# The last 256 inner columns of each expert, computed with the weights stationary and the rows moving

## The chip, the cores and the metric

The kernel runs on one core of a Trainium2 chip. The time is device microseconds of one execution. Three executions of the kernel before took 1574.29, 1574.44 and 1581.74 us; the median is 1574.44 us.

The engines are named as the profile names them: PE is the TensorE matmul stream, PEld its stream of weight loads, DVE is VectorE, ACT is ScalarE, POOL is GpSimd, SP is SyncE, whose queue issues the weight transfers.

## The reference, cut to what matters

The reference is one step of a two-layer decoder trunk for 256 prompt rows and 32 sample rows of width 1024. The second layer ends with a top-2-of-8 expert SwiGLU, and only that part is touched here:

```python
D_MODEL = 1024
D_FF = 2816
N_EXPERTS = 8
TOP_K = 2

def _swiglu(h, wg, wu, wd):
    return (jax.nn.silu(h @ wg) * (h @ wu)) @ wd

def _moe(h, router, wg, wu, wd):
    xt = h.reshape(-1, D_MODEL)
    logits = (xt @ router).astype(jnp.float32)
    top_v, top_i = lax.top_k(logits, TOP_K)
    top_w = jax.nn.softmax(top_v, axis=-1)
    gates = jnp.sum(jax.nn.one_hot(top_i, N_EXPERTS, dtype=jnp.float32) * top_w[..., None],
                    axis=1).astype(h.dtype)
    y = jnp.zeros_like(xt)
    for e in range(N_EXPERTS):
        y = y + gates[:, e:e + 1] * _swiglu(xt, wg[e], wu[e], wd[e])
    return y.reshape(shp)
```

Everything is float32. The inner width 2816 is five blocks of 512 columns and a rest of 256.

## The kernel before

Each expert works on at most 96 gathered rows (`CAP`). Each expert's weights come in 33 pieces of 1 MB (128 partitions x 2048 elements); `g` counts all 264 pieces, `i` is the piece within the expert. Pieces 0 to 19 are four pieces for each 512-column block: two halves of the gate weights, two halves of the up weights. Piece 20 is the gate weights of the last 256 columns, piece 21 the up weights of the same columns, both with all 8 blocks of 128 input rows. Pieces 22 to 32 are the down weights, 256 inner rows each.

To keep the accuracy of float32 at the speed of the rounded type float32r, every operand is split into a high part and a low rest: ACT copies a piece from the ring `ering` (8 slots) into `wH` (3 slots), DVE subtracts and writes `wL`. Each product is then three matmuls, high x high, high x low and low x high (`product`). The matmuls of one piece are issued in the order of its input blocks.

The order of the work is written out by hand. In each engine's program a loop runs over the pieces, and tables of piece numbers say behind which piece the small steps come: `SILU_AT` (ACT takes the gate sums out of PSUM bank 0 through Silu into `sgE`), `MULT_AT` (DVE multiplies bank 1, the up sums, with `sgE` into `hS`), `TRANSPOSE_AT` (PE transposes `hS` in blocks of 128 columns into bank 6 or 7, function `e_hidden`), `HID_AT` (ACT copies the transposed block as the high part into `hH`, DVE writes the low rest to `hL`). The down products use `hH` and `hL` as stationary operands and wait for `e_hl`. ACT makes the high part of piece g+2 in its step g, after piece g-1 is done, DVE the low part after it, and SP issues the transfer of piece g+8 once the low part of piece g is made (line 483).

In pieces 0 to 21 the 96 rows are the stationary operand (`xgH`, `xgL`, 128x96) and the weights move through, 512 or 256 columns at a time, so the sums come out as 96 rows x columns; that is why `hS` has to be transposed. The last block has two blocks of 128 inner columns, and its two transposes come behind piece 22.

Names of rows in the profile: line 2355 is the matmul in `product`, 2364 the transposes of `hS`, 2347 the transposes of the gathered rows, 1044 ACT's high part, 1546 DVE's low part, 1080 the Silu, 1664 the multiplication, 1085 and 1670 the high and low part of the hidden block.

Of the kernel before, what the change touches and what calls it, by code (L numbers as in the profile page):

```python
# [19 lines left out]
ALU = mybir.AluOpType  # L20
ACT = mybir.ActivationFunctionType
# [6 lines left out]
P = 128  # L28
D, DC = 1024, 8
# [9 lines left out]
E_, CAP = 8, 96  # L39
# [10 lines left out]
HRING = 3  # L50
# [4 lines left out]
def trunk_kernel(nc, a, out):  # L55

    with ExitStack() as ctx:
        def sb(name, shape, dt=F32):
            return ctx.enter_context(nc.sbuf_tensor(name, shape, dt))
# [4 lines left out]
        banks = [ctx.enter_context(nc.psum_tensor(f"bank{i}", [P, 512], F32)) for i in range(8)]  # L64
# [55 lines left out]
        wH = sb("wH", [P, HRING, SLOT], F32R)  # L120
        wL = sb("wL", [P, HRING, SLOT], F32R)
        with nc.sbuf_tensor("hrow", [P, 4, D], F32) as hrow:
            hrow = hrow[:, 1:4, :]
        hH, hL = [sb(name, [P, FC, CAP], F32R) for name in ("hH", "hL")]
# [4 lines left out]
        xgH, xgL = [sb(name, [P, DC, 2 * CAP], F32R) for name in ("xgH", "xgL")]  # L129
# [1 line left out]
        emem = sb("emem", [P, 1024])  # L131
        xtk = sb("xtk", [P, 3, D])
        yS = sb("yS", [P, D])
        sgE = sb("sgE", [P, 512])[0:CAP]
        outg = sb("outg", [P, D])
        hS = sb("hS", [P, 2, 512])[0:CAP]
        Sx = sb("Sx", [P, 3, 2 * CAP])
        Dh = nc.dram_tensor("token_rows", (T, D), F32, kind="Internal").ap()
        Dy = nc.dram_tensor("expert_rows", (E_ * CAP + 1, D), F32, kind="Internal").ap()
# [136 lines left out]
        S = {}  # L276
# [25 lines left out]
        for n in range(16):  # L302
            q = (n + 8) % 16
# [24 lines left out]
        for m, i in enumerate((1, 2, 0)):  # L328
            w = a["b_w_rkv"][0, i].rearrange("(k p) n -> p k n", p=P)
# [156 lines left out]
        SILU_AT = (2, 6, 10, 14, 18, 21)  # L486
        MULT_AT = (4, 8, 12, 16, 20, 22)
        HID_AT = (6, 10, 14, 18, 21, 23)
        TRANSPOSE_AT = (5, 9, 13, 17, 20, 22)
        BON = (6, 7, 0, 1, 2, 3, 6, 7)  # L490
        GATE_AT = (0, 4, 8, 12, 16, 20)
        UP_AT = (2, 6, 10, 14, 18, 21)
# [2 lines left out]
        def main(rd):  # L495
            return isinstance(rd, int)
# [297 lines left out]
        def _(act):  # L794
# [271 lines left out]
            def e_round(rd):  # L1066
                e_w_high(rd, 0)
                e_w_high(rd, 1)
                e_x_high(rd, 0)
                for g in range(ALL):  # L1070
                    e, i = g // EPIECES, g % EPIECES
                    if i == 0 and e:
                        e_result(rd, e - 1)
                    if i in SILU_AT:
                        q = SILU_AT.index(i)
                        act.wait_ge(S["e_piece"], rd * ALL + g)
                        if not main(rd) or 6 * e + q:
                            act.wait_ge(S["e_he"], rd * 6 * E_ + (6 * e + q))
                        w = 512 if q < 5 else 256
                        s_.activation(sgE[:, 0:w], banks[0][0:CAP, 0:w], ACT.Silu).then_inc(S["e_sg"], 1)  # L1080
                    if i in HID_AT:
                        q = HID_AT.index(i)
                        nb = 4 if q < 5 else 2
                        act.wait_ge(S["e_htr"], rd * 6 * E_ + (6 * e + q + 1))
                        s_.activation(hH[:, 4 * q:4 * q + nb, :], banks[6 + q % 2][:, 0:nb * CAP]
                                      .rearrange("p (j s) -> p j s", j=nb), ACT.Copy).then_inc(S["e_hh"], 1)
                    if i == 27 and e < E_ - 1:
                        e_x_high(rd, e + 1)
                    if main(rd) and e == LAST and i == 10:
                        act.wait_ge(S["last_sx"], 4)  # L1090
                        s_.activation(SwT, banks[2][0:CAP, 0:T], ACT.Copy).then_inc(S["last_sx"], 1)
                    if main(rd) and e == LAST and i == 24:
                        s_.activation(w7[:, 2, 0:1], eps[:, 0:1], ACT.Sqrt)
                        act.wait_ge(S["e_yout"], 16 * LAST)
                    if g + 2 < ALL:
                        e_w_high(rd, g + 2)
                if not main(rd):
                    e_result(rd, E_ - 1)
# [48 lines left out]
        def _(dve):  # L1147
# [497 lines left out]
            def e_round(rd):  # L1645
                if not main(rd):
                    e_slots(rd, 0)
                    e_index(rd, 0)
                e_w_low(rd, 0)
                e_w_low(rd, 1)  # L1650
                e_x_low(rd, 0)
                c_index(rd)
                for g in range(ALL):
                    e, i = g // EPIECES, g % EPIECES
                    if i == 0 and e:
                        e_result(rd, e - 1)
                    if i in MULT_AT:
                        q = MULT_AT.index(i)
                        w = 512 if q < 5 else 256
                        dve.wait_ge(S["e_piece"], rd * ALL + g)  # L1660
                        dve.wait_ge(S["e_sg"], rd * 6 * E_ + (6 * e + q + 1))
                        if not main(rd) or 6 * e + q >= 2:
                            dve.wait_ge(S["e_htr"], rd * 6 * E_ + (6 * e + q - 1))
                        v.tensor_tensor(hS[:, q % 2, 0:w], banks[1][0:CAP, 0:w], sgE[:, 0:w], ALU.mult) \
                            .then_inc(S["e_he"], 1)
                    if i in HID_AT:
                        q = HID_AT.index(i)
                        nb = 4 if q < 5 else 2
                        dve.wait_ge(S["e_hh"], rd * 6 * E_ + (6 * e + q + 1))
                        v.tensor_tensor(hL[:, 4 * q:4 * q + nb, :], banks[6 + q % 2][:, 0:nb * CAP]  # L1670
                                        .rearrange("p (j s) -> p j s", j=nb), hH[:, 4 * q:4 * q + nb, :].bitcast(F32),
                                        ALU.subtract).then_inc(S["e_hl"], 1)
                    if i == 5 and e < E_ - 1:
                        e_slots(rd, e + 1)
                    if i == 9 and e < E_ - 1:
                        e_index(rd, e + 1)
                    if main(rd) and e == LAST:
                        if i == 5:
                            last_slots()
                        if i in ADD_AT:  # L1680
                            add_got(ADD_AT.index(i))
                    if i == 27 and e < E_ - 1:
                        e_x_low(rd, e + 1)
                    if g + 2 < ALL:
# [42 lines left out]
        def _(pe):  # L1727
# [624 lines left out]
            def product(dst, lhs, rhs, start, stop):  # L2352

                for m, (l, r) in enumerate(((0, 0), (0, 1), (1, 0))):
                    mm = t.matmul(dst, lhs[l], rhs[r], start=(start and m == 0), stop=(stop and m == 2),  # L2355
                                  skip_group_check=True)
                return mm

            def e_hidden(rd, e, q):
                pe.wait_ge(S["e_he"], rd * 6 * E_ + (6 * e + q + 1))  # L2360
                if not main(rd) or 6 * e + q >= 2:
                    pe.wait_ge(S["e_hl"], rd * 6 * E_ + (6 * e + q - 1))
                for j in range(4 if q < 5 else 2):
                    mm = t.transpose(banks[6 + q % 2][:, CAP * j:CAP * j + CAP], hS[:, q % 2, P * j:P * j + P],  # L2364
                                     ident[0:CAP, 0:CAP])
                mm.then_inc(S["e_htr"], 1)
# [28 lines left out]
            def e_round(rd):  # L2395
# [3 lines left out]
                for g in range(ALL):  # L2399
# [9 lines left out]
                        pe.wait_ge(S["e_ya"], rd * E_ + e)  # L2409
                        pe.wait_ge(S["e_yd"], rd * E_ + e)  # L2410
                    pe.wait_ge(S["e_lo"], rd * ALL + (g + 1))
                    if i < 22:
                        kn, half = (4, i % 2) if i < 20 else (DC, 0)
                        b, w = ((i % 4) // 2, 512) if i < 20 else (i - 20, 256)
                        w2 = [x[:, g % HRING, :].rearrange("p (k n) -> p k n", k=kn) for x in (wH, wL)]
                        for k in range(kn):
                            kk = kn * half + k
                            mm = product(banks[b][0:CAP, 0:w], [x[:, kk, o:o + CAP] for x in (xgH, xgL)],
                                         [x[:, k, :] for x in w2], kk == 0, kk == DC - 1)
                    else:  # L2420
                        r = i - 22
                        pe.wait_ge(S["e_hl"], rd * 6 * E_ + (6 * e + r // 2 + 1))
                        if main(rd) and e == LAST and i >= 31:
                            mm = last_down(g)
                            if i == 32:
                                mm.then_inc(S["e_piece"], 2)
                            continue
                        for k in range(2):
                            for hf in range(2):
                                mm = down(g, k, hf)  # L2430
# [47 lines left out]
```

## Time and profile before

| | |
|---|---|
| median of three executions | 1574.44 us |
| span of the profiled execution | 1580.4 us |
| highest of the three executions, the one nearest to that span | 1581.74 us |
| PE busy / share of the span | 1531.4 us, 97% |
| DVE busy / share | 1075.8 us, 68% |
| ACT busy / share | 843.9 us, 53% |
| expert stage, first to last product | 808 to 1569 us of the span |
| transfers in the expert stage | 360 to 400 GB/s |

The busy share of PE is made of durations whose ends are modelled: the matmuls overlap, and a matmul of 512 columns that is shown with 0.39 us starts every 0.23 us. What a matmul costs is therefore read from the distance of two starts, not from its duration. The same holds for weight loads in PEld.

### The profile page before, as it was taken

The page shows a single profiled execution, that of the slowest core. Times are in us where ns is not written, and L with a number is a line of the kernel's source. Part 1 is how long each engine was busy: PE and PEld are TensorE (multiplying, and loading weights), DVE is VectorE, ACT ScalarE, POOL GpSimd, SP SyncE. Part 2 cuts the span into 40 slices and gives each one's busy share as a digit, 9 for nine tenths or more (in the row PEclk, how much of TensorE's full clock was granted, in tenths as well). Part 3 has the DMA queues.
Part 4 walks back from the last instruction along what each step waited for, and adds up shares of the span by engine and source line. Part 5 has one row for each costly group of instructions (what it writes and reads, how often), then busy time and mean ns, then how long its engine had stood idle before and what let it go on. Part 6 is the DMA issues. An engine that isn't in the chain of part 4 may idle for free.

```text
span 1580.4 us, 27011 instructions
## 1 busy us (share of the span) xinstructions
PE 1531.4 (97%) x11783; PEld 1252.3 (79%) x11783; DVE 1075.8 (68%) x1038; ACT 843.9 (53%) x813; POOL 129.2 (8%) x169
## 2 busy tenths in 40 slices
PE   7999999999899989999879999999999999999997
PEld 7999999999777789986657777777777777777774
DVE  5696465544506564212378888888988889888997
ACT  5444443333223322223167777777777777777775
POOL 0074100000100030123100000000000000000010
PEclk9999999999999999889879999999999999999999
DMA  8552675445243020024099999999999999999992
GB/s 265 171 154 63 177 224 162 152 129 160 82 136 107 27 57 4 20 49 133 2 360 381 396 379 400 382 370 363 380 385 377 369 373 383 380 368 373 385 388 99
DMA packets 249472, 377.96 MB, mean 239 GB/s; under 512 B 27401, under 2 KB 141305, under 8 KB 249058
## 3 DMA queue, kind: packets, MB, share of 16 engines
q1 hardware_dynamic: 247106, 370.04, 67.2%
q0 software_dynamic: 2032, 6.05, 1.2%
q8 instruction: 95, 1.56, 0.4%
q14 instruction: 31, 0.25, 0.1%
q10 hardware_dynamic: 208, 0.07, 0.0%
HBM read 368.34 MB, written 7.78 MB: 238 GB/s over the span
## 4 chain that ended last, share of the span: by engine, by line
PE 93%; DVE 5%; ACT 1%; issue 1%; DMA 0%; ACTq 0%; DVEq 0%
PE bank L2355 46%; PE bank L1761 23%; PE bank L1884 5%; PE bank L2030 2%; PE bank L2277 1%; PE bank L2015 1%; PE bank L2286 1%; PE bank L2364 1%; PE bank L2226 1%; PE bank L1814 1%; DVE wL L1546 1%; PE bank L2168 1%; PE bank L2296 1%; PE bank L2217 0%; PE bank L2159 0%
## 5 line engine op out<-in xcount | busy, mean ns | idle before, releaser
L1546 DVE TENSOR_TENSOR wL<-ering,wH 128x2048 fp32r<-128x2048 f32 x264 | 603.4, 2289 | 86.6 <-ACT wH L1044 85.4
L1044 ACT ACTIVATE wH<-ering 128x2048 fp32r<-128x2048 f32 x264 | 505.8, 1917 | 148.1 <-PE bank L2355 148.0
L2355 PE MATMUL bank<-wH,xgH 128*96 128x512 f32 (+1 forms) x768 | 290.4, 378 | 1.4 <-DVE xgL L1553 1.4
L2355 PE MATMUL bank<-wH,xgL 128*96 128x512 f32 (+1 forms) x768 | 287.3, 374 | 0.0
L2355 PE MATMUL bank<-wL,xgH 128*96 128x512 f32 (+1 forms) x768 | 287.2, 374 | 0.0
L2355 PEld LDWEIGHTS bank<-wH,xgH 128*96 128x96 f32 x768 | 124.4, 162 | 44.3 <-DVE xgL L1553 1.7
L2355 PEld LDWEIGHTS bank<-wH,xgL 128*96 128x96 f32 x768 | 124.4, 162 | 44.1
L2355 PEld LDWEIGHTS bank<-wL,xgH 128*96 128x96 f32 x768 | 124.6, 162 | 41.5
L2355 PE MATMUL bank<-wH,hH 128*96 128x512 f32 x352 | 139.5, 396 | 0.3 <-DVE wL L1546 0.3
L2355 PE MATMUL bank<-wH,hL 128*96 128x512 f32 x352 | 138.3, 393 | 0.0
L2355 PE MATMUL bank<-wL,hH 128*96 128x512 f32 x352 | 137.9, 392 | 0.0
L868 ACT ACTIVATE fwH<-fring 128x2048 fp32r<-128x2048 f32 (+1 forms) x38 | 64.2, 1690 | 116.6 <-PE bank L1761 116.6
L1263 DVE TENSOR_TENSOR fwL<-fring,fwH 128x2048 fp32r<-128x2048 f32 (+1 forms) x38 | 76.4, 2010 | 42.5 <-ACT fwH L868 42.5
L1761 PE MATMUL bank<-fxH,fwH 128*128 128x288 f32 x352 | 104.4, 297 | 0.0
L1761 PE MATMUL bank<-fxH,fwL 128*128 128x288 f32 x352 | 103.8, 295 | 0.0
L1761 PE MATMUL bank<-fxL,fwH 128*128 128x288 f32 x352 | 103.5, 294 | 0.0
L1884 PE MATMUL bank<-arena 128*128 128x288 f32 (+1 forms) x416 | 101.9, 406 | 0.0
L1884 PEld LDWEIGHTS bank<-arena 128*128 128x128 f32 (+1 forms) x416 | 77.5, 187 | 23.4 <-issue 0.8
L1761 PE MATMUL bank<-inH,inW 128*128 128x288 f32 x256 | 76.9, 300 | 1.0 <-DVE inL L1209 0.6
L2355 PEld LDWEIGHTS bank<-wH,hL 128*96 128x96 f32 x352 | 56.7, 161 | 24.7
L2355 PEld LDWEIGHTS bank<-wH,hH 128*96 128x96 f32 x352 | 56.8, 161 | 24.3 <-DVE wL L1546 1.1
L1761 PE MATMUL bank<-inH,lowW 128*128 128x288 f32 x256 | 75.5, 295 | 0.0
(405 smaller groups left out, 2468.6 us busy)
## 6 DMA issues: line engine op xcount, KB each, us to landing
ering<-m_w_gate SPq DMA_DIRECT2D x88, 1024.0 KB, 8.0
ering<-m_w_up SPq DMA_DIRECT2D x88, 1024.0 KB, 8.6
ering<-m_w_down SPq DMA_DIRECT2D x88, 1024.0 KB, 8.3
arena<-a_w_in SPq DMA_DIRECT2D x16, 1024.0 KB, 5.8
arena<-b_w_rkv SPq DMA_DIRECT2D x12, 1024.0 KB, 5.3
fring<-f_w_gate SPq DMA_DIRECT2D x11, 1024.0 KB, 5.4
fring<-f_w_up SPq DMA_DIRECT2D x11, 1024.0 KB, 5.3
fring<-f_w_down SPq DMA_DIRECT2D x16, 704.0 KB, 4.7
```

The costliest lines, as they stand in the source:

```text
L868: nc.scalar.activation(fw[n % FRING][0][:, 0:w], fring[:, (F_GU + n) % RING, 0:w], ACT.Copy) \
L1044: s_.activation(wH[:, g % HRING, :], ering[:, g % MRING, :], ACT.Copy).then_inc(S["e_hi"], 1)
L1263: v.tensor_tensor(fw[n % FRING][1][:, 0:w], fring[:, (F_GU + n) % RING, 0:w], fw[n % FRING][0][:, 0:w].bitcast(F32), ALU.subtract).then_in ...
L1546: v.tensor_tensor(wL[:, g % HRING, :], ering[:, g % MRING, :], wH[:, g % HRING, :].bitcast(F32), ALU.subtract).then_inc(S["e_lo"], 1)
L1761: mm = t.matmul(bank[:, 0:T], w2[l], x2[r][:, k, :], start=(start and m == 0), stop=(stop and m == 2))
L1814: mm = t.matmul(banks[c % 4][:, t0:t0 + n], vtok[0:n, i, P * c:P * c + P], w, start=False, stop=True, skip_group_check=True)
L1884: mm = t.matmul(bank, w(k), x[:, k, :], start=(k == 0), stop=(k == ks - 1))
L2015: mm = t.matmul(banks[3 * f][ch, 64 * j:64 * j + 64], MS[ch, BL, i, 8 * f + j, :], X[ch, 8 * f + j, :], start=(j == 0), stop=True, skip_gr ...
L2030: mm = t.matmul(banks[1 + 3 * f + x][ch, 64 * j:64 * j + 64], pair[x], pair[1 - x], start=(j == 0), stop=True, skip_group_check=True)
L2168: mm = t.matmul(out_[ch, :, NS * b:NS * b + NS], S0[p][ch, b, :], QR[ch, p, :, NP_ + NS * b:NP_ + NS * b + NS], start=(p % 4 == 0 and b == ...
L2226: mm = t.matmul(bank[BOTH[h2], 64 * b:64 * b + 64], S0[p][BOTH[h2], b, :], id64[BOTH[h2]], start=False, stop=True, skip_group_check=True)
L2355: mm = t.matmul(dst, lhs[l], rhs[r], start=(start and m == 0), stop=(stop and m == 2), skip_group_check=True)
```

## The change

Pieces 20 and 21 of each expert are computed the other way round. A block of 128 x 128 weights (`wH` or `wL`) is now the stationary operand and the 96 rows (`xgH` or `xgL`) move through. The sums come out as 128 inner columns x 96 rows, two such blocks side by side in the bank, which is the layout that `hH` and `hL` need. So the Silu and the multiplication of the last block run on 128x192 instead of 96x256, the two transposes behind piece 22 go, and ACT and DVE make `hH` and `hL` of this block from `hS` in SBUF instead of from PSUM. The counter `e_htr` runs to 5 per expert instead of 6, and the waits on it are renumbered.

```diff
-        TRANSPOSE_AT = (5, 9, 13, 17, 20, 22)
+        TRANSPOSE_AT = (5, 9, 13, 17, 20)
...
+                        else:
+                            s_.activation(sgF5[:, 0:2 * CAP], banks[0][:, 0:2 * CAP], ACT.Silu).then_inc(S["e_sg"], 1)
...
+                        else:
+                            act.wait_ge(S["e_he"], rd * 6 * E_ + (6 * e + 6))
+                            s_.activation(hH[:, 20:22, :], hS2[:, 1, 0:2 * CAP].rearrange("p (j s) -> p j s", j=2), ACT.Copy) \
+                                .then_inc(S["e_hh"], 1)
...
-                        if not main(rd) or 6 * e + q >= 2:
-                            dve.wait_ge(S["e_htr"], rd * 6 * E_ + (6 * e + q - 1))
+                        if q >= 2:
+                            dve.wait_ge(S["e_htr"], rd * 5 * E_ + (5 * e + q - 1))
+                        elif q == 0 and (not main(rd) or e):
+                            dve.wait_ge(S["e_htr"], rd * 5 * E_ + 5 * e)
+                        elif q and (not main(rd) or e):
+                            dve.wait_ge(S["e_hl"], rd * 6 * E_ + 6 * e)
...
+                            v.tensor_tensor(hS2[:, 1, 0:2 * CAP], banks[1][:, 0:2 * CAP], sgF5[:, 0:2 * CAP], ALU.mult) \
+                                .then_inc(S["e_he"], 1)
...
-                for j in range(4 if q < 5 else 2):
+                for j in range(4):
...
-                    if i < 22:
-                        kn, half = (4, i % 2) if i < 20 else (DC, 0)
-                        b, w = ((i % 4) // 2, 512) if i < 20 else (i - 20, 256)
-                        w2 = [x[:, g % HRING, :].rearrange("p (k n) -> p k n", k=kn) for x in (wH, wL)]
-                        for k in range(kn):
-                            kk = kn * half + k
-                            mm = product(banks[b][0:CAP, 0:w], [x[:, kk, o:o + CAP] for x in (xgH, xgL)],
-                                         [x[:, k, :] for x in w2], kk == 0, kk == DC - 1)
...
+                    elif i < 22:
+                        w2 = [x[:, g % HRING, :].rearrange("p (k n) -> p k n", k=DC) for x in (wH, wL)]
+                        for j in range(2):
+                            for k in range(DC):
+                                mm = product(banks[i - 20][:, CAP * j:CAP * j + CAP], [x[:, k, P * j:P * j + P] for x in w2],
+                                             [x[:, k, o:o + CAP] for x in (xgH, xgL)], k == 0, k == DC - 1)
```

In PE's program, where piece 20 begins behind the last 512-column matmuls of the first expert, the order before reads (name of the moving operand first where two stand behind the arrow, then the shape of the result):

```order
L2355 MATMUL bank<-wH,xgH 96x512
L2355 MATMUL bank<-wL,xgH 96x512
L2355 MATMUL bank<-wH,xgL 96x512
L2355 MATMUL bank<-wH,xgH 96x256 [waits e_lo,e_sg]
L2355 MATMUL bank<-wL,xgH 96x256
L2355 MATMUL bank<-wH,xgL 96x256
```

And now:

```order
L2370 MATMUL bank<-wH,xgH 96x512
L2370 MATMUL bank<-wL,xgH 96x512
L2370 MATMUL bank<-wH,xgL 96x512
L2370 MATMUL bank<-xgH,wH 128x96 [waits e_lo,e_sg]
L2370 MATMUL bank<-xgL,wH 128x96
L2370 MATMUL bank<-xgH,wL 128x96
```

The waits stay where they were. A piece had 24 matmuls of 256 moving columns there, and has 48 of 96 moving columns now; the same holds for piece 21.

Behind piece 22, the first of the down weights, PE's program before has the two transposes, with their wait for the multiplication (`e_he`) and for the buffer (`e_hl`):

```order
L2355 MATMUL bank<-wL,hH 96x512
L2355 MATMUL bank<-wH,hL 96x512
L2364 MATMUL bank<-ident,hS 128x96 [waits e_hl,e_he]
L2364 MATMUL bank<-ident,hS 128x96
L2355 MATMUL bank<-wH,hH 96x512 [waits e_hl,e_lo]
L2355 MATMUL bank<-wL,hH 96x512
```

Now piece 23 follows piece 22 at once:

```order
L2370 MATMUL bank<-wL,hH 96x512
L2370 MATMUL bank<-wH,hL 96x512
L2370 MATMUL bank<-wH,hH 96x512 [waits e_hl,e_lo]
L2370 MATMUL bank<-wL,hH 96x512
L2370 MATMUL bank<-wH,hL 96x512
```

On DVE and ACT the steps stand in the same places as before; only their shapes and sources differ.

## Rows read from the trace of the kernel before

**Rows 1.** Chain that ended last, from the page: share of the span.
```profile
PE 93%; DVE 5%; ACT 1%; issue 1%; DMA 0%; ACTq 0%; DVEq 0%
```

**Rows 2.** Stretches: length, busy PE, PEld, DVE, ACT, POOL (count), clock, DMA share, GB/s.
```profile
813.00:873.79 60.79, 60.79 (x305) 44.66 (x303) 51.64 (x35) 46.10 (x33) 0.91 (x1) 1.00 1.05 385
867.88:873.79 5.91, 5.91 (x54) 5.90 (x52) 5.27 (x5) 4.55 (x4) 0.00 (x0) 1.00 1.02 408
```

**Rows 3.** Waits from 800 us on: who waited for whom, us, times, longest.
```profile
ACT wH L1044 <- PE bank L2355: 148.0, 194, 4.4
...
PE bank L2355 <- DVE wL L1546: 0.3, 1, 0.3
```

**Rows 4.** Timeline of PE, first expert, pieces 20 and 21: start, length.
```profile
867.88 0.28 PE L2355 MATMUL bank<-wH,xgH 128*96 128x256 f32 x1
...
870.67 0.49 PE L2364 MATMUL bank<-ident,hS 96*128 96x96 f32 x4
870.95 0.34 PE L2355 MATMUL bank<-wH,xgH 128*96 128x256 f32 x1
871.12 0.27 PE L2355 MATMUL bank<-wL,xgH 128*96 128x256 f32 x1
...
873.79 0.39 PE L2355 MATMUL bank<-wH,hH 128*96 128x512 f32 x1
```

**Rows 5.** The same of the second expert: start of piece 20, start of piece 22.
```profile
961.99 0.28 PE L2355 MATMUL bank<-wH,xgH 128*96 128x256 f32 x1
...
968.06 0.39 PE L2355 MATMUL bank<-wH,hH 128*96 128x512 f32 x1
```

**Rows 6.** Weight loads of the whole span by form: busy, mean ns of one, idle before.
```profile
L2355 PEld LDWEIGHTS bank<-wL,xgH 128*96 128x96 f32 x768 | 124.6, 162 | 41.5
...
L1761 PEld LDWEIGHTS bank<-fxL,fwH 128*128 128x128 f32 x352 | 66.3, 188 | 0.0
...
L2364 PEld LDWEIGHTS bank<-ident,hS 96*128 96x128 f32 x176 | 20.0, 141 | 6.4 <-DVE hS L1664 0.2
```

**Rows 7.** Timeline of PEld: float32r loads right behind each other, first 128, then 96 columns.
```profile
137.87 0.19 PEld L1810 LDWEIGHTS bank<-bsH,onesR 128*128 128x128 f32 x1
137.98 0.19 PEld L1811 LDWEIGHTS bank<-bsL,onesR 128*128 128x128 f32 x1
...
870.92 0.16 PEld L2355 LDWEIGHTS bank<-wH,xgH 128*96 128x96 f32 x1
871.00 0.17 PEld L2355 LDWEIGHTS bank<-wL,xgH 128*96 128x96 f32 x1
```

**Rows 8.** Timeline of PE: 128-column float32 loads with 8 moving columns each.
```profile
791.50 0.37 PE L2315 MATMUL bank<-emem,ones 128*128 128x8 f32 x2
791.72 0.37 PE L2315 MATMUL bank<-emem 128*128 128x8 f32 x2
```

**Rows 9.** Timeline of PE, first expert, the two transposes behind piece 22.
```profile
876.56 0.33 PE L2364 MATMUL bank<-ident,hS 96*128 96x96 f32 x2
876.67 0.46 PE L2355 MATMUL bank<-wH,hH 128*96 128x512 f32 x1
876.97 0.39 PE L2355 MATMUL bank<-wL,hH 128*96 128x512 f32 x1
877.20 0.39 PE L2355 MATMUL bank<-wH,hL 128*96 128x512 f32 x1
```

**Rows 10.** Timeline of PE, last expert, down weights.
```profile
1561.09 0.40 PE L2355 MATMUL bank<-wH,hL 128*96 128x512 f32 x1
1561.76 0.48 PE L2355 MATMUL bank<-wH,hH 128*96 128x512 f32 x1 [0.28 <-DVE wL L1546]
```

**Rows 11.** Timeline of PE: transposes of the gathered rows, 128 stationary and 96 moving columns.
```profile
1451.24 0.83 PE L2347 MATMUL bank<-ident,xrow 96*128 96x96 f32 x8
1451.85 0.45 PE L2355 MATMUL bank<-wH,hH 128*96 128x512 f32 x1
```

**Rows 12.** Timeline of PE at 778 us, and its stretch with the granted clock.
```profile
778.08 7.95 PE L2296 MATMUL bank<-arena 128*128 128x8 f32 x48 [6.60 <-DVE arena L388]
...
778.10:785.80 7.70, 7.70 (x47) 7.68 (x48) 0.00 (x0) 0.00 (x0) 0.00 (x0) 0.50 0.00 0
```

More of the change, by code:

```diff
@@ L133, in trunk_kernel @@
         yS = sb("yS", [P, D])
-        sgE = sb("sgE", [P, 512])[0:CAP]
+        sgF5 = sb("sgE", [P, 512])
+        sgE = sgF5[0:CAP]
         outg = sb("outg", [P, D])
-        hS = sb("hS", [P, 2, 512])[0:CAP]
+        hS2 = sb("hS", [P, 2, 512])
+        hS = hS2[0:CAP]
         Sx = sb("Sx", [P, 3, 2 * CAP])
@@ L1078, in e_round @@
                             act.wait_ge(S["e_he"], rd * 6 * E_ + (6 * e + q))
-                        w = 512 if q < 5 else 256
-                        s_.activation(sgE[:, 0:w], banks[0][0:CAP, 0:w], ACT.Silu).then_inc(S["e_sg"], 1)
+                        if q < 5:
+                            s_.activation(sgE, banks[0][0:CAP, :], ACT.Silu).then_inc(S["e_sg"], 1)
+                        else:
+                            s_.activation(sgF5[:, 0:2 * CAP], banks[0][:, 0:2 * CAP], ACT.Silu).then_inc(S["e_sg"], 1)
                     if i in HID_AT:
                         q = HID_AT.index(i)
[L1083 to L1086, printed above, removed]
+                        if q < 5:
+                            act.wait_ge(S["e_htr"], rd * 5 * E_ + (5 * e + q + 1))
+                            s_.activation(hH[:, 4 * q:4 * q + 4, :], banks[6 + q % 2][:, 0:4 * CAP]
+                                          .rearrange("p (j s) -> p j s", j=4), ACT.Copy).then_inc(S["e_hh"], 1)
+                        else:
+                            act.wait_ge(S["e_he"], rd * 6 * E_ + (6 * e + 6))
+                            s_.activation(hH[:, 20:22, :], hS2[:, 1, 0:2 * CAP].rearrange("p (j s) -> p j s", j=2), ACT.Copy) \
+                                .then_inc(S["e_hh"], 1)
                     if i == 27 and e < E_ - 1:
@@ L1658, in e_round @@
                         q = MULT_AT.index(i)
-                        w = 512 if q < 5 else 256
                         dve.wait_ge(S["e_piece"], rd * ALL + g)
                         dve.wait_ge(S["e_sg"], rd * 6 * E_ + (6 * e + q + 1))
-                        if not main(rd) or 6 * e + q >= 2:
-                            dve.wait_ge(S["e_htr"], rd * 6 * E_ + (6 * e + q - 1))
-                        v.tensor_tensor(hS[:, q % 2, 0:w], banks[1][0:CAP, 0:w], sgE[:, 0:w], ALU.mult) \
-                            .then_inc(S["e_he"], 1)
+                        if q >= 2:
[4 more added lines that the diff above has]
+                            dve.wait_ge(S["e_hl"], rd * 6 * E_ + 6 * e)
+                        if q < 5:
+                            v.tensor_tensor(hS[:, q % 2, :], banks[1][0:CAP, :], sgE, ALU.mult).then_inc(S["e_he"], 1)
+                        else:
+                            v.tensor_tensor(hS2[:, 1, 0:2 * CAP], banks[1][:, 0:2 * CAP], sgF5[:, 0:2 * CAP], ALU.mult) \
+                                .then_inc(S["e_he"], 1)
                     if i in HID_AT:
@@ L1668, in e_round @@
                         nb = 4 if q < 5 else 2
+                        src = banks[6 + q % 2] if q < 5 else hS2[:, 1]
                         dve.wait_ge(S["e_hh"], rd * 6 * E_ + (6 * e + q + 1))
-                        v.tensor_tensor(hL[:, 4 * q:4 * q + nb, :], banks[6 + q % 2][:, 0:nb * CAP]
+                        v.tensor_tensor(hL[:, 4 * q:4 * q + nb, :], src[:, 0:nb * CAP]
                                         .rearrange("p (j s) -> p j s", j=nb), hH[:, 4 * q:4 * q + nb, :].bitcast(F32),
@@ L2411, in e_round @@
                     pe.wait_ge(S["e_lo"], rd * ALL + (g + 1))
-                    if i < 22:
-                        kn, half = (4, i % 2) if i < 20 else (DC, 0)
-                        b, w = ((i % 4) // 2, 512) if i < 20 else (i - 20, 256)
-                        w2 = [x[:, g % HRING, :].rearrange("p (k n) -> p k n", k=kn) for x in (wH, wL)]
-                        for k in range(kn):
-                            kk = kn * half + k
-                            mm = product(banks[b][0:CAP, 0:w], [x[:, kk, o:o + CAP] for x in (xgH, xgL)],
-                                         [x[:, k, :] for x in w2], kk == 0, kk == DC - 1)
+                    if i < 20:
+                        w2 = [x[:, g % HRING, :].rearrange("p (k n) -> p k n", k=4) for x in (wH, wL)]
+                        for k in range(4):
+                            kk = 4 * (i % 2) + k
+                            mm = product(banks[(i % 4) // 2][0:CAP, :], [x[:, kk, o:o + CAP] for x in (xgH, xgL)],
+                                         [x[:, k, :] for x in w2], kk == 0, kk == DC - 1)
+                    elif i < 22:
[4 more added lines that the diff above has]
+                                             [x[:, k, o:o + CAP] for x in (xgH, xgL)], k == 0, k == DC - 1)
                     else:
```

## The prediction, made before the changed kernel ran

> **What bounds the kernel now.** I read the chain of work that ended last first. It is PE for 93% of the span [rows 1], so PE is the engine to count on unless the stage of the change is another case. The stretches say it is not: from 813 to 873.79 us, the first expert at full clock, PE is busy for the whole 60.79 us, DVE for 51.64 and ACT for 46.10 [rows 2]. Modelled ends could hide a gap there, so I read the waits next. ACT waits 148.0 us for PE to free the `wH` slots, and PE waits 0.3 us in all for DVE's low parts [rows 3]. The transfers run at 385 GB/s, but nothing in the stage waits for them. So PE is the bound and the others follow. Whatever PE's stream of matmuls gets longer or shorter by in pieces 20 and 21 is what the kernel gets longer or shorter by, eight times over.
>
> What the reader is to see in the timeline is the pace. Piece 20 of the first expert starts at 867.88 us and the transposes behind it at 870.67: 24 matmuls in 2.79 us, 0.116 us each, with 256 moving columns, 0.45 ns a column. The weight load in front of each is shown with 162 ns [rows 6], more than that pace, so loads and matmuls overlap, and with 256 columns the moving side sets the pace. The question of this change is which side sets it when the stationary operand grows from 96 to 128 columns and the moving one shrinks from 256 to 96.
>
> **What goes.** In the first expert the stretch from piece 20 to piece 22 is 873.79 - 867.88 = 5.91 us [rows 4]; in the second 968.06 - 961.99 = 6.07 us [rows 5]. The eight experts alternate between these two, mean 5.99. The four transposes between the pieces take 870.95 - 870.67 = 0.28 us, and the first matmul behind them 0.17 instead of 0.12 (871.12 - 870.95) [rows 4]; these 0.33 us stay. So 48 matmuls cost 5.66 us an expert, and they go.
>
> The two transposes behind piece 22 go too: from 876.56 to 876.97 is 0.41 us for them and one matmul of 512 columns, which else takes 0.23 (877.20 - 876.97) [rows 9]. That is 0.18 us an expert, 1.4 us in all.
>
> **What comes.** 96 matmuls an expert instead of 48, each with its own load of 128 float32r columns. The moving side would take 96 x 0.45 = 0.044 us. The load takes longer. The trace has no float32r matmul with fewer than 256 moving columns, so the cost of the pair is bounded from the nearest rows:
> - Two float32r loads that stand right behind each other start 0.11 us apart with 128 columns (137.87 and 137.98) and 0.08 us apart with 96 (870.92 and 871.00) [rows 7]. The load port is free again after that time, though a load is shown with 188 and 162 ns [rows 6].
> - Plain float32 matmuls with 128-column loads and only 8 moving columns, so nothing on the moving side, go at (791.72 - 791.50)/2 = 0.11 us [rows 8].
> - The lowest pace of a pair of the new shape (128 stationary, 96 moving) is that of the transposes: 8 in 1451.85 - 1451.24 = 0.61 us, 0.076 us each [rows 11]. But their load is a different one: 141 ns for 128 columns where the float32r load takes 188 [rows 6].
> - The upper end is a load that hides behind nothing: 0.11 + 0.044 = 0.154 us.
>
> I take 0.111 us: it is the only pace that two independent places show for a load of this size, and the moving 0.044 us fits under it. 96 x 0.111 = 10.66 us, against 5.66: +5.00 us an expert, +40.0 us in all. A quarter of the moving columns is saved (9216 instead of 12288), but they are no longer what the time goes by; twice as many and a third wider loads are.
>
> **What lies beside it and costs nothing.** The Silu, the multiplication and the two halves of `hH` and `hL` change shape on ACT and DVE; those engines have 15 and 9 us to spare in 61 [rows 2], and longer pieces 20 and 21 give them more. The wait of ACT for `e_he` instead of `e_htr` stands in front of its high part of piece 25 only; the multiplication it waits for is made by DVE as soon as piece 21 and the Silu are done, and the first down piece that reads this block is the eleventh, piece 32, nine pieces of about 2.8 us later. If that cover were gone the cost would be one ACT step, under 1 us an expert. The renumbered waits on `e_htr` and `e_hl` are for things done pieces earlier. SP issues its transfers by DVE's low parts, so while pieces 20 and 21 take 5.3 us instead of 2.8 it slows down; the ring holds eight pieces and the stage was not waiting for transfers.
>
> In the last expert PE is once held up by DVE's low part: 1561.76 - 1561.09 = 0.67 us instead of 0.23 [rows 10], since DVE also adds the gathered results there. Five more microseconds in pieces 20 and 21 let DVE catch up: -0.4 us.
>
> **The sum.** +40.0 - 1.4 - 0.4 = +38.2 us. The rows come from an execution with a span of 1580.4 us, which lies 1.3 us under the highest of the three times, 1581.74; for that execution the sum gives 1619.9. The stage of the change had full clock throughout, so the sum is the same for the others, and on the median of 1574.4 it gives 1612.6 us. I say 1612.
>
> The Trainium skill, "TensorE: Matmul & The Clock Gate", section "Back-to-back issue gap", gives a sustained 81 ns for each pair of load and matmul at 128 columns. Of the float32r load the trace shows another figure, 0.11 us for 128 columns [rows 7]. By the page's 81 ns the pieces would take 7.8 us an expert, and the kernel would end near 1590 us, in the neighbourhood of the first rival.
>
> **Rivals.**
> - *The pair goes at the pace of the transposes, 0.076 us.* 96 x 0.076 = 7.3 us, +1.6 - 0.18 an expert, +11 us in all: about 1586 us. For it: the same shape. Against it: the loads of the transposes are shown 47 ns shorter than float32r ones with as many columns [rows 6], and two float32r loads are 0.11 us apart [rows 7].
> - *The load hides altogether and the moving columns set the pace (the other side).* 96 x 0.044 = 4.2 us instead of 5.66, -1.5 - 0.18 an expert, -13 us: about 1561 us. This decides from the point where a load of 128 columns takes less than 0.044 us. For it: at 256 columns the load is hidden completely. Against it: rows 7 and 8, both 0.11 us. No row shows a load with 128 columns in under 0.07.
> - *Load and matmul don't overlap when both are short.* 96 x 0.154 = 14.8 us, +9.1 - 0.18 an expert, +71 us: about 1645 us. For it: no row with such a short float32r stream. Against it: in rows 8 each load starts while the previous matmul runs, and in rows 4 0.116 us holds a load of 0.08 and 256 moving columns of about 0.11, which would be 0.19 one after the other. The Trainium skill, on the same page, section "The mechanism" of Part 3, says that a load overlaps matmuls in flight only when the row group differs; by that rule this rival would be the forecast. Here load and matmul both use all 128 rows and do overlap, so the trace disagrees with it.
> - *The clock falls in the new pieces.* Where 128-column loads came with 8 moving columns each, at 778 us, the granted clock was 0.50 (1.2 GHz), and 32 such loads and 16 of 32 columns took 7.95 us, about 0.22 us for the large ones [rows 12]. 96 x 0.22 = 21 us, +15 an expert, +122 us: about 1696 us. Against it: PE had been idle for 6.6 us ahead of that stretch, with full moving streams around the new pieces there is no such gap, and each new load comes with 96 moving columns instead of 8.
> - *The change doesn't move the time*, since something else than PE sets it: about 1574. PE's missing waits speak against it [rows 3].
>
> **How the numbers follow.** Chances: load-bound at 0.109 to 0.116 us 0.80, the pace of the transposes or a pace between 0.07 and 0.10 us 0.07, hidden load 0.04, no overlap (or a pace well over 0.12) 0.06, clock 0.02, nothing moves 0.01. A pace from 0.109 to 0.116 gives +36.7 to +42 us: 1611 to 1616. I widen this for what loads of freshly written `wH` and `wL` may cost beside 385 GB/s of transfers, to 1600 to 1628, which holds about 0.82; with the part of the second and third cases that reaches in, the range need not go further. What a measurement of this kernel can tell from no change is about 0.5%, 8 us. Faster by more than that: the hidden load alone, 0.04. Within it: 0.02. Slower: 0.94.
>
> **What would show it.** In the profile after, the pace of the new matmuls (128 stationary, 96 moving) is the whole matter: starts 0.11 us apart, with PEld starts as far apart, and pieces 20 and 21 together 10.8 to 11.2 us instead of 5.91 to 6.07. The granted clock stays 1.00 in the expert stage. The matmul behind piece 22 follows at 0.23 us without transposes. The waits of ACT for PE grow by some 40 us, those of PE for DVE stay near nothing. The prediction is wrong if the new starts lie under 0.10 or over 0.12 us apart, if the clock falls in these pieces, or if PE gets a new wait in front of piece 23 or 32.

## The result and the profile after

The changed kernel takes 1658.8 us (median of four, 1654.0 to 1670.5) against 1574.4 on the same chip: ratio 1.052, 95% interval 1.048 to 1.055. I had forecast 1612 us, 1600 to 1628. The direction was right, the size was not: +84 us instead of +38.

The kernel before has two times, about 1574 and 1582 us, with a mean granted clock of 0.984 and 0.978; the profile before is of the second kind. The profiled execution of the changed kernel took 1657.5 us with a span of 1655.8, so against its like, 1581.7, the change costs 75.8 us.

The chain that ended last is PE again, for 94% of the span after 93% [rows 1]. The new matmuls (first group) and their loads (second group) in the timeline of the first expert, start and length:

```profile
868.64 0.21 PE L2370 MATMUL bank<-xgH,wH 128*128 128x96 f32 x1
868.68 0.27 PE L2370 MATMUL bank<-xgL,wH 128*128 128x96 f32 x1
868.80 0.27 PE L2370 MATMUL bank<-xgH,wL 128*128 128x96 f32 x1
868.91 0.28 PE L2370 MATMUL bank<-xgH,wH 128*128 128x96 f32 x1
869.02 0.28 PE L2370 MATMUL bank<-xgL,wH 128*128 128x96 f32 x1
```

```profile
868.75 0.19 PEld L2370 LDWEIGHTS bank<-xgH,wL 128*128 128x128 f32 x1
868.86 0.19 PEld L2370 LDWEIGHTS bank<-xgH,wH 128*128 128x128 f32 x1
868.97 0.19 PEld L2370 LDWEIGHTS bank<-xgL,wH 128*128 128x128 f32 x1
```

Both streams go at 0.11 us, the pace that rows 7 and 8 had shown. Ten microseconds later the same matmuls look different:

```profile
877.84 0.27 PE L2370 MATMUL bank<-xgH,wL 128*128 128x96 f32 x1
877.95 0.28 PE L2370 MATMUL bank<-xgH,wH 128*128 128x96 f32 x1
878.06 0.33 PE L2370 MATMUL bank<-xgL,wH 128*128 128x96 f32 x1
878.19 0.41 PE L2370 MATMUL bank<-xgH,wL 128*128 128x96 f32 x1
878.41 0.41 PE L2370 MATMUL bank<-xgH,wH 128*128 128x96 f32 x1
878.62 0.41 PE L2370 MATMUL bank<-xgL,wH 128*128 128x96 f32 x1
```

From 878.1 us on they start 0.21 us apart. The stretches say why. Each line gives start and end, length, busy time of PE, PEld, DVE, ACT and POOL (with counts), granted clock, DMA share, GB/s. The first is piece 20, the second piece 21, the third the start of the down weights, the fourth nearly the whole expert stage:

```profile
868.64:873.93 5.29, 5.29 (x49) 5.29 (x48) 4.54 (x3) 1.92 (x1) 0.00 (x0) 1.00 1.03 410
874.25:880.97 6.72, 6.72 (x52) 6.72 (x50) 2.85 (x2) 2.50 (x3) 0.00 (x0) 0.79 1.03 409
880.97:884.97 4.00, 4.00 (x11) 2.65 (x12) 2.13 (x2) 2.16 (x2) 0.00 (x0) 0.50 0.98 387
820.00:1650.00 830.00, 827.20 (x3980) 613.50 (x3978) 670.63 (x436) 551.51 (x396) 19.89 (x13) 0.95 0.92 333
```

The kernel before had clock 1.00 over the whole stage, 820 to 1570 us:

```profile
820.00:1570.00 750.00, 749.04 (x3604) 542.32 (x3603) 664.49 (x429) 546.97 (x384) 14.59 (x13) 1.00 1.00 369
```

So once in every expert the clock falls from 2.4 to 1.2 GHz (0.50), in five of them for 6.8 us and in three for 13.7. Pieces 20 and 21 with the transposes between them, in the first, second, fifth and last expert:

```profile
868.64:880.97 12.33, 12.33 (x102) 12.33 (x100) 7.39 (x5) 4.53 (x4) 0.00 (x0) 0.88 1.03 409
971.10:983.49 12.39, 12.39 (x102) 12.39 (x100) 7.43 (x5) 4.54 (x4) 0.00 (x0) 0.88 0.83 294
...
1278.82:1294.79 15.97, 15.97 (x102) 15.97 (x100) 7.39 (x5) 4.54 (x4) 0.00 (x0) 0.67 0.77 279
...
1593.00:1609.11 16.11, 16.11 (x101) 16.10 (x100) 8.63 (x6) 4.54 (x4) 2.16 (x1) 0.67 1.00 375
```

The eight stretches sum to 110.9 us; before they were 8 x 5.99 = 47.9 [rows 4, 5]; the forecast was 8 x 10.99 = 87.9. The low clock thus cost about 23 us inside them. It also outlasts them: behind each stretch the down weights run at 0.43 us a matmul instead of 0.23 until the clock is back (PE's timeline, first expert):

```profile
881.47 0.63 PE L2370 MATMUL bank<-wL,hH 128*96 128x512 f32 x1
881.90 0.63 PE L2370 MATMUL bank<-wH,hL 128*96 128x512 f32 x1
```

A mean clock of 0.957 over 1655.8 us is 142 us at half clock; 0.978 over 1580.4 is 70. The eight falls alone add up to 75 us; ahead of 800 us both profiles have 55. Where the clock is low the paces are about double (0.21 instead of 0.11, 0.43 instead of 0.23), so half of the 72 us more is lost, 36 us. 38 forecast and 36 from the clock make 74 of the 75.8.

### The profile page after: what moved, and what is told of

The parts are those of the page before. It is cut to its first block, busy times and chain, and to the rows that moved or that the text cites. A ratio compares the mean times of both kernels' runs of the same rounds, so it can differ in the third digit from the quotient of the medians.

```text
span 1655.8 us, 27739 instructions
## 1 busy us (share of the span) xinstructions
PE 1606.8 (97%) x12151; PEld 1322.9 (80%) x12151; DVE 1077.6 (65%) x1038; ACT 844.0 (51%) x813; POOL 134.5 (8%) x169
## 4 chain that ended last, share of the span: by engine, by line
PE 94%; DVE 4%; ACT 1%; issue 1%; DMA 0%; ACTq 0%; DVEq 0%
PE bank L2370 48%; PE bank L1776 22%; PE bank L1899 5%; PE bank L2045 2%; PE bank L2030 1%; PE bank L2292 1%; PE bank L2301 1%; PE bank L2379 1%; PE bank L2241 1%; PE bank L1829 1%; DVE wL L1554 1%; PE bank L2183 1%; PE bank L2311 0%; PE bank L2232 0%; PE bank L2174 0%
## 5 line engine op out<-in xcount | busy, mean ns | idle before, releaser
L1046 ACT ACTIVATE wH<-ering 128x2048 fp32r<-128x2048 f32 x264 | 505.7, 1916 | 209.3 <-PE bank L2370 209.3
L2370 PE MATMUL bank<-wH,xgH 128*96 128x512 f32 x640 | 254.1, 397 | 1.8 <-DVE xgL L1561 1.8
L2370 PE MATMUL bank<-wH,xgL 128*96 128x512 f32 x640 | 251.5, 393 | 0.0
L2370 PE MATMUL bank<-wL,xgH 128*96 128x512 f32 x640 | 251.3, 393 | 0.0
L2370 PE MATMUL bank<-wH,hH 128*96 128x512 f32 x352 | 145.1, 412 | 0.3 <-DVE wL L1554 0.3
L2370 PE MATMUL bank<-wL,hH 128*96 128x512 f32 x352 | 142.5, 405 | 0.0
L2370 PEld LDWEIGHTS bank<-wH,xgL 128*96 128x96 f32 x640 | 103.6, 162 | 44.2 <-issue 0.3
L2370 PEld LDWEIGHTS bank<-wH,xgH 128*96 128x96 f32 x640 | 103.7, 162 | 43.9 <-DVE xgL L1561 2.0
L2370 PEld LDWEIGHTS bank<-wL,xgH 128*96 128x96 f32 x640 | 103.7, 162 | 41.2
L2370 PE MATMUL bank<-xgH,wL 128*128 128x96 f32 x256 | 80.7, 315 | 0.0
L2370 PE MATMUL bank<-xgL,wH 128*128 128x96 f32 x256 | 80.4, 314 | 0.0
```

Of the source, the lines that this page charges most:

```text
L1046: s_.activation(wH[:, g % HRING, :], ering[:, g % MRING, :], ACT.Copy).then_inc(S["e_hi"], 1)
```

## The experiments

Two chips ran them. On the first (the runs with 192 columns, with two loads, with the pieces apart and with half of the contraction) the kernel before had a median of 1581.9 us in 13 runs, on the second (the others) 1581.7 in 11. Where a run had a clock of 0.984 or more it is compared with 1574. The expectations add to 1574, so their times in us have to be read some 8 us higher beside these medians. Theory A: the forecast sum is right at full clock, and the rest is the clock, which falls because too few columns move while the loads set the pace. A stretch with 96 moving columns in each load is called sparse below.

**192 moving columns, same loads.**

```diff
-                                mm = product(banks[i - 20][:, CAP * j:CAP * j + CAP], [x[:, k, P * j:P * j + P] for x in w2],
-                                             [x[:, k, o:o + CAP] for x in (xgH, xgL)], k == 0, k == DC - 1)
+                                mm = product(banks[i - 20][:, WIDE * j:WIDE * j + WIDE], [x[:, k, P * j:P * j + P] for x in w2],
+                                             [x[:, k, o - left(e):o - left(e) + WIDE] for x in (xgH, xgL)], k == 0, k == DC - 1)
```

(Only the matmul is shown. `left(e)` is 0 or WIDE - CAP; Silu and multiplication read the 96 wanted columns of each half. The first expert's rows are copied once into the other slot.)

> The changed kernel with 192 moving columns instead of 96 in pieces 20 and 21: the rows of the other expert's slot move along and their sums are not used (for the first expert the slot holds a copy of its own rows). Loads, their number and their 128 columns stay. 192 moving columns take 0.086 us, still less than the 0.111 us of a load, so the pace of the loads is unchanged. Theory A (the part of the time that the prediction lacked is the granted clock, and it falls because too few columns move per load): the clock stays 1.00 in the expert stage and the time is the predicted sum, 1574 + 38 = 1612 us (1608 to 1618). Rival B (the clock falls because of the stream of 128-column float32r loads, whatever moves): it falls as in the changed kernel, 1650 to 1670 us. Rival C (the missing part is not the clock but waits or slower pieces elsewhere): 1650 to 1670 us at a full clock.

Measured: 1621.1 us, ratio 1.025 (1.021 to 1.028). That lies above the 1608 to 1618 of the expectation. Compared with its like, at clock 0.978, it is 1621.2 against 1581.9, +39.3. The timeline of PE and the stretch of the whole stage:

```profile
867.70 0.27 PE L2384 MATMUL bank<-xgL,wH 128*128 128x192 f32 x1
867.82 0.28 PE L2384 MATMUL bank<-xgH,wL 128*128 128x192 f32 x1
867.93 0.27 PE L2384 MATMUL bank<-xgH,wH 128*128 128x192 f32 x1
```

```profile
820.00:1610.00 790.00, 788.89 (x3972) 582.05 (x3970) 666.43 (x431) 548.02 (x388) 15.79 (x13) 1.00 0.96 349
```

Twice the moving columns at the same pace of 0.11 us, the clock at 1.00, and the kernel is 37 us faster than the changed one. The eight stretches of pieces 20 and 21 take 11.04 us each, 88.3 in all, where the forecast had 87.9 and the changed kernel took 110.9. The +39.3 us are theory A's 38 nearly to the microsecond. This rules out B and C: the same loads in the same number don't lower the clock when more columns move beside them.

**128 moving columns.** The same edit with WIDE = 128.

> As the run with 192 moving columns, but 128: 0.057 us of moving columns in each load of 0.111 us. The load sets the pace, so at a full clock the time is before + 39 us, as with 192 columns. Whether the clock holds is open. If it takes clearly more moving columns than 96 (192 held it): falls as in the changed kernel, before + 70 to 80 us. If 96 was just too few: no falls, before + 39 us. I expect the second with 0.6.

Measured: 1620.4 us, ratio 1.025 (1.023 to 1.027); four of its runs 1620.0 to 1621.6, one at clock 0.985 1612.7, which is +39 in both cases. The profile shows no falls:

```profile
820.00:1600.00 780.00, 779.03 (x3930) 575.14 (x3928) 657.89 (x423) 541.12 (x380) 15.51 (x13) 1.00 0.96 350
```

A third more moving columns are enough here. The time doesn't depend on whether 128 or 192 columns move, since the load sets the pace.

**96 columns loaded.**

```diff
-                                mm = product(banks[i - 20][:, CAP * j:CAP * j + CAP], [x[:, k, P * j:P * j + P] for x in w2],
+                                mm = product(banks[i - 20][0:96, CAP * j:CAP * j + CAP], [x[:, k, P * j:P * j + 96] for x in w2],
```

> The changed kernel with only 96 of the 128 columns of each block loaded (the last 32 inner columns of each block are left out): 96 loads of 96 columns an expert with 96 moving columns each. Theory A (the load sets the pace, by its columns): two such loads were 0.08 us apart before, 96 x 0.083 = 8.0 us, +(8.0 - 5.66 - 0.18) x 8 = +17 us. The moving columns are 0.043 of 0.083 us, as dense as with 128 moving columns and a full load, so the clock does as there: full, before + 17 us, or with falls before + 45 us. Rival E (any float32r pair with so few moving columns takes 0.111 us whatever the load): before + 39 us or more.

The sums of 32 columns of each block are missing, so the result is incomplete. Measured: 1599.5 us, ratio 1.012 (1.008 to 1.015); at clock 0.978 1602.2 against 1581.7, +20. Timeline and stage:

```profile
863.25 0.25 PE L2370 MATMUL bank<-xgL,wH 128*96 128x96 f32 x1
863.33 0.25 PE L2370 MATMUL bank<-xgH,wL 128*96 128x96 f32 x1
863.42 0.25 PE L2370 MATMUL bank<-xgH,wH 128*96 128x96 f32 x1
863.50 0.25 PE L2370 MATMUL bank<-xgL,wH 128*96 128x96 f32 x1
```

```profile
820.00:1585.00 765.00, 764.03 (x3952) 558.21 (x3951) 661.02 (x426) 544.32 (x382) 19.99 (x13) 1.00 0.98 359
```

The pace is 0.085 us, so the load sets it by its columns, and rival E is out. 96 x 0.085 = 8.2 us gives +19, measured +20. The 96 moving columns are those of the changed kernel, but they come every 0.085 us instead of every 0.111, and in this run the clock stays.

**Two loads for each block instead of three.**

```diff
-                                mm = product(banks[i - 20][:, CAP * j:CAP * j + CAP], [x[:, k, P * j:P * j + P] for x in w2],
-                                             [x[:, k, o:o + CAP] for x in (xgH, xgL)], k == 0, k == DC - 1)
+                                dst = banks[i - 20][:, 2 * CAP * j:2 * CAP * j + 2 * CAP]
+                                t.matmul(dst.rearrange("p (m s) -> p m s", m=2), w2[0][:, k, P * j:P * j + P], xg2[:, :, k, o:o + CAP],
+                                         start=(k == 0), stop=False, skip_group_check=True)
+                                mm = t.matmul(dst[:, 0:CAP], w2[1][:, k, P * j:P * j + P], xgH[:, k, o:o + CAP],
+                                              start=False, stop=(k == DC - 1), skip_group_check=True)
```

(Only the matmuls are shown. `xg2` holds `xgH` and `xgL` one behind the other; Silu and multiplication read the first of the two sums of each block.)

> The changed kernel with two loads for each 128x128 block instead of three: the block of wH is loaded once and the high and low parts of the rows move through it together (192 columns, two sums side by side), the block of wL is loaded with 96 moving columns. The addition of the second sum is left out. 64 loads an expert instead of 96. Theory A: loads set the pace, 64 x 0.111 = 7.1 us instead of 10.66, 288 moving columns in 0.22 us keep the clock at 1.00: 1574 + 8 x (7.1 - 5.66 - 0.18) = 1584 us (1580 to 1592). Rival B (load stream lowers the clock): 1600 to 1615 us.

Measured: 1594.0 us, ratio 1.009 (1.006 to 1.012), just above the expected 1580 to 1592. At clock 0.978 it is 1594.1 against 1581.9, at 0.984 1586.1 against 1574.0, +12 both times, where +10 was expected. The clock of the stage is 1.00, so rival B is out here too. A pair of loads takes 0.22 us (862.15 to 862.37):

```profile
862.15 0.32 PE L2444 MATMUL bank<-xg,wH 128*128 128x192 f32 x1
862.31 0.23 PE L2446 MATMUL bank<-xg,wL 128*128 128x96 f32 x1
862.37 0.32 PE L2444 MATMUL bank<-xg,wH 128*128 128x192 f32 x1
```

A third fewer loads take back 27 of the 39 us that the swap costs at full clock. It is the best form of the swap that was tried, and still slower than before, without the addition that it leaves out.

**The two sparse pieces apart.**

```diff
-            elif i < 22:
-                w = a["m_w_up" if i == 21 else "m_w_gate"][0, e].rearrange("(k p) n -> p k n", p=P)
+            elif i in (20, 25):
+                w = a["m_w_up" if i == 25 else "m_w_gate"][0, e].rearrange("(k p) n -> p k n", p=P)
...
-        MULT_AT = (4, 8, 12, 16, 20, 22)
-        HID_AT = (6, 10, 14, 18, 21, 23)
+        MULT_AT = (4, 8, 12, 16, 20, 26)
+        HID_AT = (6, 10, 14, 18, 21, 27)
```

(PE's program, the transfers and the order of the down pieces are changed to match.)

> The changed kernel with the same work in another order: piece 20 (gate, last block), then four pieces of down weights, then the up piece of the last block, then the other seven down pieces. The two stretches with 96 moving columns are 5.3 us each with 11 us of 512-column matmuls between them, instead of 11 us on end. Theory A with the length of the sparse stretch mattering (in the changed kernel piece 20 always ran at full clock, 5.30 us, and the clock was low in piece 21): no or few falls, 1612 to 1625 us. Rival D (each sparse stretch brings a fall of its own, however short): sixteen falls of 6.8 us at half clock, +55 us on the 1612, 1650 to 1680 us.

Measured: 1653.2 us, ratio 1.045 (1.042 to 1.049). Theory A's addition that the length decides fell: 1612 to 1625 was expected of it. The time lies in rival D's range of 1650 to 1680, but its "each stretch" doesn't hold either. Four of the sixteen sparse stretches, the two of the first expert and the two of the sixth:

```profile
867.34:872.63 5.29, 5.29 (x49) 5.29 (x48) 4.54 (x3) 1.92 (x1) 0.00 (x0) 1.00 1.05 401
884.09:889.38 5.29, 5.29 (x50) 5.29 (x48) 4.01 (x2) 1.91 (x1) 0.00 (x0) 1.00 1.04 394
1381.20:1387.53 6.33, 6.33 (x50) 6.32 (x48) 4.58 (x3) 1.92 (x1) 0.00 (x0) 0.83 1.01 387
1401.12:1406.93 5.81, 5.81 (x50) 5.81 (x48) 4.03 (x2) 1.92 (x1) 0.00 (x0) 0.91 1.01 360
```

The first two experts had no fall, the other six two each, with the same instructions. Ten of the twelve falls lasted 6.8 us and two 3.4, which makes 75 us, the same as in the eight falls of the changed kernel: taking the pieces apart gained nothing. So a stretch of 5.3 us can bring a fall or not. What decides is not in the program's order; no run shows what it is.

**Half of the contraction.**

```diff
-                            for k in range(DC):
+                            for k in range(4):
```

> The changed kernel with only the first four of the eight 128-row blocks in pieces 20 and 21 (the other half of these products is left out): 48 loads an expert in 5.3 us instead of 96 in 10.7. Theory A with the length mattering: hardly a fall, 1574 + 8 x (5.33 - 5.66 - 0.18) = 1570 us (1566 to 1580). Rival D (a sparse stretch of any length brings a fall): eight falls of 6.8 us at half clock, up to +27 us, 1590 to 1600 us.

Measured: 1580.1 us, ratio 0.998 (0.997 to 1.000). At clock 0.978 it is 1580.1 against 1581.9, -2 where the sum gives -4: the same number of loads as before, 128 columns each, costs about what the 256 moving columns cost. In this profile the clock fell once in the stage, in the last expert, just behind the sparse stretch, for 3.4 us, though all eight stretches have the same 5.6 us with the transposes in their middle. That is the "hardly a fall" of theory A, and the eight falls of rival D didn't come. But beside the run before, with twelve falls in sixteen stretches of 5.3 us, length alone doesn't decide.

**The form before with 96 moving columns.**

```diff
-                            mm = product(banks[b][0:CAP, 0:w], [x[:, kk, o:o + CAP] for x in (xgH, xgL)],
-                                         [x[:, k, :] for x in w2], kk == 0, kk == DC - 1)
+                            m = w if i < 20 else CAP
+                            mm = product(banks[b][0:CAP, 0:m], [x[:, kk, o:o + CAP] for x in (xgH, xgL)],
+                                         [x[:, k, 0:m] for x in w2], kk == 0, kk == DC - 1)
```

> The kernel before (rows stationary, transposes kept) with 96 instead of 256 moving columns in pieces 20 and 21 (the other 160 inner columns are left out): 48 loads of 96 columns an expert. Theory A: the load of 96 columns now sets the pace, 48 x 0.083 = 4.0 instead of 5.66 us, -13 us in all. Rival E: the pace stays near 0.11 us, 48 x 0.111 = 5.3 us, -3 us. If moving columns set the pace, 48 x 0.044 = 2.1 us, -28 us.

Measured: 1576.5 us, ratio 0.997 (0.994 to 0.999), -4 us where theory A expected -13. The number is that of rival E, but the reason is not. The pace is 0.085 us as expected, and then PE waits:

```profile
869.40 0.25 PE L2355 MATMUL bank<-wL,xgH 128*96 128x96 f32 x1
869.49 0.25 PE L2355 MATMUL bank<-wH,xgL 128*96 128x96 f32 x1
869.97 0.55 PE L2364 MATMUL bank<-ident,hS 96*128 96x96 f32 x4 [0.23 <-DVE hS L1664]
...
874.94 0.40 PE L2355 MATMUL bank<-wH,hL 128*96 128x512 f32 x1
875.56 0.38 PE L2364 MATMUL bank<-ident,hS 96*128 96x96 f32 x2 [0.22 <-DVE hS L1664]
...
1528.22 0.25 PE L2355 MATMUL bank<-wH,xgL 128*96 128x96 f32 x1
1529.51 0.71 PE L2355 MATMUL bank<-wH,hH 128*96 128x512 f32 x1 [1.04 <-DVE wL L1546]
1530.02 0.63 PE L2355 MATMUL bank<-wL,hH 128*96 128x512 f32 x1
1530.44 0.63 PE L2355 MATMUL bank<-wH,hL 128*96 128x512 f32 x1
```

The next start behind 869.49 would be 869.57, it is 869.97; behind 874.94 it would be 875.17, it is 875.56. Some 0.8 us an expert are lost to the multiplication on DVE, half of the 1.6 that the faster pieces win (5.66 - 48 x 0.085). In the last expert two things are added, in the last three lines: PE waits 1.04 us for DVE's low part, and from 1528.9 us on, within that wait, the clock is low for 3.4 us. So this run, too, has a fall behind a stretch of 96 moving columns every 0.085 us, which the run with 96 columns loaded had not. PE bounds this stage by a small margin: a change that shortens pieces 20 and 21 gets only a part of it.

**The changed kernel once more.**

> The changed kernel once more, beside many runs of the kernel before on the same chip, since the kernel before has two times, 1574 and 1582 us, which go with a mean granted clock of 0.984 and 0.978. By theory A every execution of the changed kernel differs from one of before by 39.5 us of work at full clock and by half of the additional low-clock time: 1650 to 1662 us, with the mean clock between 0.954 and 0.961, +68 to +78 us against the executions of before at clock 0.978.

Measured: 1658.2 us, ratio 1.049 (1.047 to 1.051); three runs of 1657.7 to 1660.1 at clock 0.955 to 0.957, one of 1651.6 at 0.960. Against 1581.7 that is +76; times and clocks are inside the expectation. At 1651.6 us the mean clock of 0.960 means 132 us at half clock, against 70 in the kernel before: 31 us lost, and 1581.7 + 39.3 + 31 = 1652. The same working gives 1673 us for the slowest run of the first occasion, with a clock of 0.948; it took 1670.5.

## Why the prediction was wrong

- **PE is the bound, 0.111 us a pair, twice as many pairs: right.** The chain, the pace of both streams and the runs with 192 and 128 moving columns show it. The sum was +38.2 us; where the stage kept its full clock (192 columns) +39.3 was measured.
- **The transposes behind piece 22 go, nothing else gets in the way: right.** PE got no new wait in front of piece 23 or 32. ACT's waits for PE grew from 148.0 [rows 3] to 209.3 us, by more than the forecast 40, as PE took longer.
- **The clock: the step that failed.** The prediction said "The stage of the change had full clock throughout, so the sum is the same for the others", and gave the rival of a falling clock 0.02. Its reasons were that PE had been idle ahead of the low clock at 778 us [rows 12], that no such gap is near the new pieces, and that 96 columns move with each load instead of 8. The clock fell all the same, with PE issuing without a gap: in five experts in the middle of piece 21, in the three with the long falls already between pieces 20 and 21. The Trainium skill, "TensorE: Matmul & The Clock Gate", section "Why this matters for your kernels", ties drops in mid-kernel to idle gaps of PE between bursts; in this trace no gap precedes them. The term that the sum put at nothing is 36 us, and the runs at more moving columns show that it is this term and no other.
- **The reason against the falling clock: refuted by the trace of the kernel before.** From about 662 to 687 us its clock was at 0.50 too, and there PE has no wait at all from 650 to 700 us. It issued matmuls, most of them with 64 or 8 moving columns, one behind the other. So a low clock did not need idle time ahead of it, as the prediction took from the 778 us stretch. The middle of this fall, columns as above:

```profile
664.00:684.00 20.00, 20.00 (x284) 18.00 (x284) 1.48 (x3) 1.57 (x3) 2.08 (x2) 0.50 0.01 2
```

- **The price of that rival was too high as its chance was too low.** It took half clock for all new matmuls, +122 us. In fact piece 20 ran at full clock in all eight experts. The low clock covered a part of piece 21, in three experts all of it, and some of the down weights.
- **The other rivals: rightly small.** No pair went under 0.11 us with a load of 128 columns, and load and matmul overlap. What the hidden load would have brought was probably too high, too: in the last but one run, whose pieces were about as short, PE waited 0.4 us an expert for the multiplication in front of the transposes between pieces 20 and 21, which the swap keeps. That would have been an estimated 3 of the 13 us; no run shows it.

Between 75.8 and 84.4 lie 7.3 us from the two times of the kernel before, whose profile is of the 1582 us kind while the median of its first runs is of the 1574 us kind, and 1.3 us between the median of the changed kernel and its profiled run. Beside more runs of the kernel before, on the second chip, the difference of the medians is 76.5.

No version that makes all the products beat the kernel before. The two that are not slower, half of the contraction and the form before with 96 moving columns, leave out a part of them. The step that failed, the full clock, is thus shown; why a fall comes in one expert and not in the next stays open.

## What to carry to other kernels

Before swapping the operands, count loads as well as columns: pairs of a float32r load and a short matmul start 0.111 us apart with 128 loaded columns and 0.085 with 96, about 0.88 ns a loaded column. So here a short moving stream behind a full 128-column load was paid at the price of the load, with 96 rows as with 192. Then look at how densely columns move in the new stretch, since a PE that is never idle can still lose half its clock, and look in the trace before for stretches where that has happened already. If it must be so, let one load serve more moving columns: two loads for three products took back 27 of 39 us here, without the addition of the second sum.

## What the runs showed that was not expected

- With no idle time on PE, 128-column loads every 0.111 us and 96 moving columns each, the granted clock of the changed kernel fell to 0.50 once in every expert. In the profiles with 128 or 192 moving columns at the same pace it never did. With 96 every 0.085 us it never did in one run, and once in the other, where PE also waited 1.04 us for DVE. The low clock outlasts its cause: the 512-column matmuls behind the stretch, as dense as any, went at 0.43 us for up to 4 us in the first expert.
- The same instructions had a fall in some experts and none in others (the run with the pieces apart). So the time of such a kernel moves with the number and length of the falls: the changed one took from 1651.6 to 1670.5 us, with a mean clock from 0.960 to 0.948.
- The two times of the kernel before are probably of the same kind; none of its profiles is of the 1574 us kind. In a stage of small matmuls, far from the change, the mean clock of the stretch from 655 to 690 us is 0.66 in the profile before (first row) and 0.95 in the profile with 128 moving columns, which is of the faster kind (second row). The profile with two loads, of the faster kind as well, has 0.95 there too:

```profile
655.00:690.00 35.00, 35.00 (x695) 32.84 (x691) 3.46 (x5) 6.79 (x12) 6.06 (x5) 0.66 0.05 10
```

```profile
655.00:690.00 35.00, 35.00 (x930) 32.76 (x927) 5.71 (x10) 8.71 (x15) 8.61 (x7) 0.95 0.09 18
```
